# All three weight chunks of a GEMM's tail are waited for ahead of its first matmul

## The reference

```
merged = sigmoid(gate_a) * (o_a @ w_br_a) + sigmoid(gate_b) * (o_b @ w_br_b);  x = x + merged @ w_out
# second block, twice (l = 0, 1):
mix = concat([a, f]) @ w_o[l];   h = layer_norm(ALPHA * h + mix, ln1_g[l], ln1_b[l])
h = layer_norm(ALPHA * h + swiglu(h, w_gu[l], w_down[l]), ln2_g[l], ln2_b[l])
```

## Time and profile before

| | us |
|---|---|
| median of 3 runs | 2006.64 (2006.56 to 2007.01) |
| the profiled execution's own time | 2006.64 |
| its span in the profile | 2005.4 |
| PE busy | 1838.4 (92% of the span) |
| DVE busy | 958.5 (48%) |
| ACT busy | 777.3 (39%) |

### The profile page before, as it was taken

How to read it: one execution, slowest core, us unless ns; L and a number is a source line. 1 busy time by engine, 2 the same in 40 slices (tenths; PEclk the granted TensorE clock), 3 DMA queues, 4 the chain that set the end, 5 groups by cost and what they waited for, 6 DMA issues and landing times.

```text
span 2005.4 us, 26563 instructions
## 1 busy us (share of the span) xinstructions
PE 1838.4 (92%) x10396; PEld 1449.7 (72%) x10396; DVE 958.5 (48%) x1881; ACT 777.3 (39%) x1436; POOL 394.9 (20%) x438
## 2 busy tenths in 40 slices
PE   7999999996998754998999999999999999999997
PEld 6888777785544424776778888787876778888786
DVE  4458776663311015968454433234868454333234
ACT  3344476221433234665253233115566252332212
POOL 1019155102222111243011111000233012111001
PEclk9999999996999996998999999999998999999999
DMA  4244200576999983211323333232211233333231
GB/s 162 80 113 126 95 2 2 168 286 242 381 383 401 394 308 125 74 53 43 105 85 100 100 95 95 89 100 70 77 64 43 84 95 98 101 95 95 87 103 53
DMA packets 134884, 264.43 MB, mean 132 GB/s; under 512 B 11616, under 2 KB 92128, under 8 KB 122464
## 3 DMA queue, kind: packets, MB, share of 16 engines
q1 hardware_dynamic: 116320, 228.35, 33.1%
q10 hardware_dynamic: 13312, 25.90, 3.8%
q0 software_dynamic: 5120, 8.40, 1.3%
HBM read 254.22 MB, written 16.78 MB: 135 GB/s over the span
## 4 chain that ended last, share of the span: by engine, by line
PE 54%; DMA 9%; DVE 7%; ACT 3%; issue 2%; POOL 1%; PEld 1%; PEldq 0%; ACTq 0%; POOLq 0%; SPq 0%; DVEq 0%
PE b L507 15%; PE b L508 15%; PE b L509 15%; DMA m<-in_w_gate_up 6%; PE b L2023 3%; ACT m L622 2%; DVE m L2736 1%; DMA m<-in_w_down 1%; PE b L2561 1%; PE b L2048 1%; PE b L2543 1%; PE b L2529 1%; DMA s_h<-m 1%; ACT m L690 1%; DVE m L694 1%
## 5 line engine op out<-in xcount | busy, mean ns | idle before, releaser
L507 PE MATMUL b<-m,m 128*128 128x512 f32 (+3 forms) x2060 | 782.0, 380 | 28.4 <-DVE m L636 8.8
L508 PE MATMUL b<-m,m 128*128 128x512 f32 (+3 forms) x2060 | 772.6, 375 | 0.0
L509 PE MATMUL b<-m,m 128*128 128x512 f32 (+3 forms) x2060 | 772.5, 375 | 0.0
L493 DVE TENSOR_TENSOR m<-m,m 128x1024 fp32r<-128x1024 f32 (+1 forms) x212 | 278.2, 1319 | 497.5 <-ACT m L483 496.6
L507 PEld LDWEIGHTS b<-m,m 128*128 128x128 f32 x2060 | 392.6, 191 | 105.8 <-issue 22.1
L509 PEld LDWEIGHTS b<-m,m 128*128 128x128 f32 x2060 | 392.4, 190 | 67.5
L508 PEld LDWEIGHTS b<-m,m 128*128 128x128 f32 x2060 | 393.1, 191 | 64.1
L483 ACT ACTIVATE m<-m 128x1024 fp32r<-128x1024 f32 (+1 forms) x236 | 245.7, 1048 | 484.2 <-PE b L509 458.0
L2986 POOL TENSOR_TENSOR m<-m,m 128x512 fp32r<-128x512 f32 x44 | 71.1, 1636 | 422.1 <-ACT m L2932 422.1
L2023 PE MATMUL b<-m,m 128*64 128x256 f32 x1024 | 126.7, 390 | 27.5 <-DMA m<-in_w_gate_up 26.2
L2023 PEld LDWEIGHTS b<-m,m 128*64 128x64 f32 x1024 | 73.6, 139 | 78.9 <-issue 38.6
(11 more groups left out here) (339 smaller groups left out, 1896.2 us busy)
## 6 DMA issues: line engine op xcount, KB each, us to landing
m<-in_w_gate_up SPq DMA_DIRECT2D x64, 1024.0 KB
m<-in_w_gu SPq DMA_DIRECT2D x88, 512.0 KB, 3.5
m<-in_w_down SPq DMA_DIRECT2D x32, 1024.0 KB
m<-in_w_in SPq DMA_DIRECT2D x48, 512.0 KB, 3.8
m<-in_w_down SPq DMA_DIRECT2D x44, 512.0 KB, 3.7
m<-in_w_in SPq DMA_DIRECT2D x20, 448.0 KB, 3.6
m<-in_w_o SPq DMA_DIRECT2D x16, 512.0 KB, 3.8
s_gt<-m ACTq DMA_DIRECT2D x16, 256.0 KB, 2.1
```

The lines of the kernel that those rows point to most:

```text
L493: e.tensor_tensor(flat(wlo[HX[i]], i), flat(raw[RX[i][0]], i), fr(flat(whi[HX[i]], i)), ALU.subtract).then_inc(sem("w_lo"), 1)
L507: e.matmul(out, xh, yh, start=start, stop=False, skip_group_check=True)
L508: e.matmul(out, xh, yl, start=False, stop=False, skip_group_check=True)
L509: return e.matmul(out, xl, yh, start=False, stop=stop, skip_group_check=True)
```

## The change

In `gemm_tail` the weight chunks were fetched (that is, waited for) as the first token tile came to each: chunk one, 6 matmuls, chunk two, 6 matmuls, chunk three, 6 matmuls. Now all are waited for ahead of the loop. The matmuls, their order and operands, and all that other engines do stay the same.

```diff
-            w = []
+            w = [chunk(e, i) for i, _ in units]
             for t in range(NT):
                 sl = slice(t * P, t * P + P)
                 for n, (i, ks) in enumerate(units):
-                    if t == 0:
-                        w.append(chunk(e, i))
                     hi, lo = w[n]
```

## The result

The changed kernel took 2024.15 us (median of 4, 2023.49 to 2026.70) beside 2006.60 for the kernel before (median of 4, 2002.20 to 2007.01). The ratio is 1.009 with a 95% interval of 1.0075 to 1.0104, so it is slower by 15 to 21 us. 2024.1 was forecast. Its profiled execution took 2024.15 us, with a span of 2022.9. All 22 executions of it on record took 2018.76 to 2027.61 us, with a median of 2024.0.

A forecast was written before the change was run, and what follows sets the result against it. PE, busy for 92% of the span, was taken to bound the kernel. 2006.64 us plus 13.5 for five tail waits with restarts and 4 for lowered clock gave 2024.1 us, with an 8-in-10 range of 2019.0 to 2028.5.

The forecast's parts named there:

- PE bounds the kernel: Whole kernel: PE busy 92% of the span; time it loses where nothing else is late is lost for the whole.
- The two waits removed cost nothing: In each of five tails, the two removed waits of PE for `w_lo` were said to cost nothing.
- 2.63 us per tail plus 0.07 to restart: Ahead of each of five tails: PE waits for the third chunk's halving, then restarts; 13.5 us in all.
- 2.47 us of idle time: Ahead of each tail: PE's expected idle time in the new wait, 2.63 - 0.16 us.
- Wout counted in full: At the tail wout: its delay was taken to reach the end, though DVE reaches tile 0 late there.
- Three slow stretches of five: Behind the new waits: lowered clock in three of five tails, 1.5 us each, 4.5 us rounded down to 4.
- the discount for tile 1: Clock term: 4.5 us rounded down to 4, as tile 0's norm partly covers a slow stretch in tile 1.
- The sum: Whole kernel: 2006.64 + 13.5 + 4 = 2024.1 us, 0.87% slower.
- A: Tails: the wait alone, clock staying up in all or all but one; 2020.1 us, with one drop 2021.6; chance 0.26.
- B: Tails: the clock drops in every one, adding 7.5 us to the wait; 2027.6 us; chance 0.17.
- C: Behind the tails: the norm train hides the wait; 2006.6 us, or 2002 to 2005; chance 0.06 together with D.
- D: Ahead of the tails: third chunk already ready, so the wait falls through; 2006.6 us; chance 0.06 together with C.

The follow-up runs named there:

- e5: Kernel before with the early wait for all chunks in the tail wout alone, the other four as before: 2008.47 us beside 2004.56, ratio 1.0018.
- e6: Kernel before with the early wait for all chunks in the last tail dn1 alone: 2009.07 us, ratio 1.0029.
- e1: Kernel before with chunks one and two waited for ahead of each tail, the third when due: 2006.62 us beside 2005.13, ratio 1.0006.
- e3: Changed kernel with 11 filler matmuls keeping PE busy while it waits ahead of each tail: 2019.53 us beside 2005.13 for the kernel before, ratio 1.0071.
- e4: Changed kernel with the last chunk of wo0, dn0, wo1 and dn1 in the spare buffers: 2020.07 us beside 2005.13 for the kernel before, ratio 1.0079.
- e8: Changed kernel run once more, unaltered, on the chip of other runs: 2026.89 us beside 2004.56 for the kernel before, ratio 1.0118.
- e7: Kernel before plus 14 filler matmuls ahead of w_down's first matmul and 8 ahead of w_o's first: 2002.97 us beside 2004.56, ratio 0.9989.
- e9: Kernel before plus 14 fillers ahead of w_down and 8 where w_o really waits, its third chunk: 2001.13 us beside 2006.17, ratio 0.9976.

## Why the prediction was right, point by point

- **PE bounds the kernel, and its idle time in the tails is a loss for the whole.** Held. e5 and e6 show it for the first and the last tail alone.
- **The two waits removed cost nothing, the second chunk is ready.** Held: e1 is as before.
- **2.63 us per tail plus 0.07 to restart, 13.5 us.** The tail's first matmul is late by 2.72 in each tail and 13.6 in all, in both traces of the changed kernel and in e3. Two small sizes were off, in opposite directions: from the halving's end to PE it takes 0.14 us, where 0.05 was read from a group of two halvings, so the wait term is 2.72 and not 2.63; and the restart leaves 0.03 to 0.07, not always 0.07. Where the clock stayed up the tail costs 2.75 to 2.79 in all beside 2.70. 2.47 us of idle time were expected, 2.56 are seen.
- **Wout counted in full.** Held (e5). That SP's transfers start later too is seen: `in_w_down` is issued at 460.95 in the kernel before, at 463.82 in e5 (2.87 later; PE is late by 2.85 there) and at 463.14 in the changed kernel (2.19; PE 2.18).
- **Three slow stretches of five, 4 us.** The trace of the changed kernel has three, for 1.4 (wout), 1.6 and 1.6 us, 4.6 in all. The second trace of it has four, and those of e5 and e6 have one each; with e4, whose wout had none, that is 9 of 13. My three of five was a fair count and partly luck, and the discount for tile 1 wasn't needed. One of its reasons was an accident of one trace: behind the 2.42 us of idle time at 87.59 the clock stayed up in the kernel before, but at that same place, ahead of anything that was changed, it fell in 7 of the 12 traces, as here in e6:

```profile
86.59 0.64 PE L903 MATMUL b<-m,m 128*96 128x128 f32 x4 [2.41 <-POOL m L739]
87.70:90.70 3.00, 3.00 (x10) 2.65 (x9) 1.84 (x2) 1.00 (x2) 0.20 (x1) 0.50 0.39 141
```

- **The sum.** 13.5 + 4 was forecast; the tails made 18.46, other places -0.95 in that execution. The hit to 0.1 us is luck: the other places vary by some us between executions, as the spread of the kernel before (2000.6 to 2009.9) and of the changed one (2018.8 to 2027.6) shows, and in e8, on another chip, the changed kernel was 22 us above.
- **The rivals.** A (clock stays up) and B (all five drop) are both refuted as a rule, each by the tails of the other sort; for the total of a single execution they are not, see the spread. C (the norm hides it) falls with DVE's idle time ahead of tile 0, 2.8 to 4.4 us longer, and with e6. D (idle edit) falls with the five waits. The Trainium skill, "TensorE: Matmul & The Clock Gate", section "A second HAM failure mode: psum-queue depth-cycling", describes a clock that swings where PE is often idle for a short time between groups of matmuls, and a throughput that suffers from it. The traces agree that short idle times can lower the clock and that this costs beside the wait itself (1.4 to 1.6 us each); it does not happen each time (9 of 13).

## What to carry to other kernels

A wait placed at first use can be the one that hides a hand-over: before hoisting it, read the time at which its producer ends, and who had to free the buffer for that producer. Count a wait on PE ahead of dense matmuls as its length plus, in most cases, about 1.5 us of half clock (for the waits of 2 to 3.4 us seen here; behind those of 1.20 us there was none). One trace doesn't tell whether the clock falls at a place: compare several executions. And a spare buffer that looks unused belongs to some stage: giving it away moves the stall to there (e4).

## What the runs showed of the hardware

- Useless matmuls in a wait that can't be removed are worth their trouble: 14 of them in a gap of 3.43 us, or 8 in one of 1.98, kept the granted clock at 1.00 behind it (6 of 6 in e7 and e9) and saved 1.5 to 1.6 us each in e9, against a trace in which it had fallen. Placed some 14 us ahead of the wait, where PE was busy, 8 of them cost their own 1.81 us (e7).
- The same idle time at the same place of an unchanged stretch of the program may or may not lower the clock. Without fillers at these places, it fell behind 15 of 20 waits of 1.98 us in w_o (ten traces, e7 and e9 left out), behind 16 of 20 waits of 3.43 us in w_down, behind 7 of 12 waits of 2.4 to 2.5 us at L903, and behind none of 12 waits of 1.53 to 1.56 us at L599. In w_o of layer 0, 1.98 us of idle time were followed by 0.50 in the kernel before, and by 1.00 in e1:

```profile
976.00 0.50 PE L507 MATMUL b<-m,m 128*128 128x512 f32 x1 [1.98 <-DVE m L493]
976.00:979.00 3.00, 3.00 (x13) 2.50 (x14) 2.82 (x3) 0.42 (x1) 0.00 (x0) 1.00 0.55 157
```

- The spread of several us between executions of one kernel (the one before: 2000.6 to 2009.9) has a second source beside the clock. In the trace of e1, PE waits twice for DVE's L2490 in layer 1's attention, at places where the kernel before did not wait in its own trace, with the clock at 1.00:

```profile
1445.28 0.50 PE L507 MATMUL b<-m,m 128*128 128x512 f32 x1 [1.42 <-DVE m L2490]
1453.80 0.50 PE L507 MATMUL b<-m,m 128*128 128x512 f32 x1 [0.85 <-DVE m L2490]
```

The shift grows by 2.2 us there. The same two waits stand in the traces of e3, e4, e6, e7 and e8, and in none of the other six. What decides whether they happen was not tried.
